# A decoder layer with two mixers: twenty pairs of weight columns formed by seven block products in a stage of their own

## What is computed

```python
h = rms_norm(x, g_norm[l]) * (1.0 + scale) + shift
proj = h @ w_in[l]
xa, va, oa, za, ia, fa, qa, ka, vat, zb, ga, gb = jnp.split(proj, split_at, axis=-1)
xc = silu(causal_depthwise_conv(xa, w_conv[l], b_conv[l]))
q_m, k_m = xc_h @ w_q_mlstm, xc_h @ w_k_mlstm * (MLSTM_HEAD_DIM ** -0.5)
h_m = mlstm_chunkwise(q_m, k_m, v_m, ia + b_igate[l], fa + b_fgate[l])
h_m = rms_norm(sigmoid(oa) * h_m, g_mlstm_head[l]) + skip_mlstm[l] * xc
y_m = (h_m * silu(za)) @ w_out_mlstm[l]
qh, kh = partial_rotary(qa, positions), partial_rotary(ka, positions)
o_g, lse_g = dilated_window_attention(qh, kh, vh, window, dilation)   # 3 groups x 4 heads
o_a = sum over the groups of softmax(lse) * o_g
y_a = (o_a * silu(zb)) @ w_out_attn[l]
merged = sigmoid(ga) * y_m + sigmoid(gb) * y_a
x = rms_norm(x + gate * (merged @ w_out[l]), g_final)
```

## Time and profile before

| | busy in the span of 1565.1 us | share |
|---|---|---|
| TensorE, matmul | 1552.8 us | 99% |
| TensorE, weight load | 1219.1 us | 78% |
| VectorE | 816.0 us | 52% |
| ScalarE | 510.7 us | 33% |
| GpSimd | 368.4 us | 24% |
| DMA | 117.19 MB | 75 GB/s on the mean |

### The profile page before, as it was taken

How to read it: one execution, slowest core, us unless ns; L and a number is a source line. 1 busy time by engine, 2 the same in 40 slices (tenths; PEclk the granted TensorE clock), 3 DMA queues, 4 the chain that set the end, 5 groups by cost and what they waited for, 6 DMA issues and landing times.

```text
span 1565.1 us, 17246 instructions
## 1 busy us (share of the span) xinstructions
PE 1552.8 (99%) x6717; PEld 1219.1 (78%) x6717; DVE 816.0 (52%) x1360; ACT 510.7 (33%) x925; POOL 368.4 (24%) x206
## 2 busy tenths in 40 slices
PE   8999999999999999999999999999999999999998
PEld 7777788877778887777888777788877777777776
DVE  7685446455454645434464543446396415343476
ACT  7644223432322343132235313222542336111122
POOL 0221111122111112211111211111128764221441
PEclk9888888888888888888888888888888888888888
DMA  9211011143111114210001421011041305332432
GB/s 335 93 55 44 27 28 28 35 141 95 61 41 41 41 37 146 67 41 27 28 27 28 136 67 41 27 27 28 28 136 40 121 1 201 100 102 95 158 121 94
DMA packets 51818, 117.19 MB, mean 75 GB/s; under 512 B 20753, under 2 KB 20881, under 8 KB 51734
## 3 DMA queue, kind: packets, MB, share of 16 engines
q1 hardware_dynamic: 47642, 103.23, 20.3%
q10 hardware_dynamic: 2976, 8.80, 1.6%
q0 software_dynamic: 1120, 4.06, 0.9%
HBM read 100.64 MB, written 15.43 MB: 74 GB/s over the span
## 4 chain that ended last, share of the span: by engine, by line
PE 98%; DMA 1%; ACT 1%; SPq 0%; DVE 0%; issue 0%; ACTq 0%; DVEq 0%
PE banks L568 27%; PE banks L567 27%; PE banks L569 27%; PE banks L858 2%; PE banks L868 2%; PE banks L819 2%; PE banks L825 2%; PE banks L877 1%; PE banks L805 1%; PE banks L817 1%; PE banks L558 1%; PE banks L846 1%; PE banks L530 1%; DMA raw_lo<-in_x 1%; PE banks L835 1%; PE banks L807 1%
## 5 line engine op out<-in xcount | busy, mean ns | idle before, releaser
L567 PE MATMUL banks<-h_hi,whi 128*128 128x512 f32 x1000 | 427.8, 428 | 0.4 <-ACT szb L939 0.3
L707 POOL TENSOR_TENSOR wlo<-wraw,whi 128x1024 fp32r<-128x1024 f32 x77 | 194.4, 2524 | 970.8 <-ACT whi L955 952.9
L569 PE MATMUL banks<-h_hi,wlo 128*128 128x512 f32 x1000 | 417.3, 417 | 0.0
L568 PE MATMUL banks<-h_lo,whi 128*128 128x512 f32 x1000 | 417.1, 417 | 0.0
L569 PEld LDWEIGHTS banks<-h_hi,wlo 128*128 128x128 f32 x1000 | 191.9, 192 | 58.6
L567 PEld LDWEIGHTS banks<-h_hi,whi 128*128 128x128 f32 x1000 | 193.0, 193 | 55.2 <-issue 1.2
L568 PEld LDWEIGHTS banks<-h_lo,whi 128*128 128x128 f32 x1000 | 192.8, 193 | 54.1
L955 ACT ACTIVATE whi<-wraw 128x1024 fp32r<-128x1024 f32 x75 | 78.9, 1052 | 97.8 <-PE banks L569 97.8
L568 PE MATMUL banks<-wlo,h_hi 128*128 128x512 f32 x240 | 100.2, 418 | 0.0
L569 PE MATMUL banks<-whi,h_lo 128*128 128x512 f32 x240 | 100.2, 417 | 0.0
L567 PE MATMUL banks<-whi,h_hi 128*128 128x512 f32 x240 | 99.9, 416 | 0.0
(11 more groups left out here) (382 smaller groups left out, 2708.5 us busy)
## 6 DMA issues: line engine op xcount, KB each, us to landing
wraw<-in_w_all SPq DMA_DIRECT2D x92, 512.0 KB, 3.6
s_wada<-in_w_ada_cols SPq DMA_DIRECT2D x16, 512.0 KB, 6.5
raw_lo<-in_x SPq DMA_DIRECT2D x8, 512.0 KB, 9.2
mlstm_branch<-xc SPq DMA_DIRECT2D x8, 512.0 KB, 3.8
qm<-group_weights SPq DMA_DIRECT2D x8, 512.0 KB, 6.2
part<-in_w_ada_gate SPq DMA_DIRECT2D x16, 256.0 KB, 3.4
sig_c<-in_w_all SPq DMA_DIRECT2D x8, 512.0 KB, 4.5
um_lo_raw<-mlstm_branch SPq DMA_DIRECT2D x8, 512.0 KB, 4.9
```

The lines of the kernel that those rows point to most:

```text
L567: t_.matmul(out, w_hi, x_hi, start=first, stop=False)
L568: t_.matmul(out, w_hi, x_lo, start=False, stop=False)
L569: return t_.matmul(out, w_lo, x_hi, start=False, stop=last)
L707: nc.gpsimd.tensor_tensor(wlo[:, hi, :], wraw[:, q % 2, :], whi[:, hi, :].bitcast(F32), ALU.subtract).then_inc(w_split, 1)
```

## The change

A new stage, `blocks`, stands between `setup` and `mix`. In it 20 pairs of weight columns are formed by seven block products each: the 5 gates m = 3 to 7, the 12 pairs of query and key (one for each attention head), and the 3 conv inputs of the heads 1 to 3. The conv input of head 0 and the gate m = 2 are made plainly ahead of them; the gates m = 0 and 1 stay in the merge. TensorE has 7 x 12 = 84 matmuls of 512 columns for it. GpSimd has 4 combinations and 7 splits for a pair, ScalarE 7 roundings, 1 copy and 2 final copies, VectorE 7 additions, and for a query and key pair the rotation of 32 partitions for both at once. A result of 1 MB goes through `fin` to DRAM (`sig_d`, `qk_d`, `xa_d`), and the heads and the merge load it from there.

A head now has 10 chunks (4 of tokens, 3 of values, 2 of ZA, 1 of ZB) and the fold. The small matmuls stand behind each group of 12 matmuls: 24 steps u per head from the first value chunk on, with the mLSTM from u = 3, the attention from u = 5, the normalisation at u = 19 and the turning of the output at u = 21. The `sums` and the rope tables are made in `blocks`, and what the heads use comes later or earlier in the program accordingly.

```diff
-MAIN = 18
...
+VO, VG, ZA, ZB = 0, 4, 7, 9
+MAIN = 10
...
+PRODUCTS = 7
+ORDER = (5, 1, 2, 4, 6, 7, 3)
+PARTS = ("u2", "u4", "c11", "c22", "v", "c21", "c12")
+GATES = KT - PLAIN - 1
+QK0 = GATES
+XA0 = QK0 + HEADS * GROUPS
+PAIRS = XA0 + HEADS - 1
+TOTAL = PRODUCTS * PAIRS
...
+def blocks(nc, a, sem, ps, T):
...
+        def load_pair(r):
+            if r == 0:
+                sp.wait_ge(w_split, 6)
+            elif r >= 2:
+                sp.wait_ge(s_split, PRODUCTS * (r - 1))
+                sp.wait_ge(s_added, 4 * (r - 1))
+            for c in range(2):
+                sp.dma_start(raw[r % 2][:, c, :], a["w_all"][PAIRS0 + 2 * r + c]).then_inc(pair_in[r % 2], 16)
+
+        def store(r):
+            sp.wait_ge(fin_done, 2 * r + 2)
+            sp.dma_start(dest(r), fin[:, r % 2]).then_inc(fin_out[r % 2], 16)
...
+        def combine(j, x, y, op):
+            nc.gpsimd.tensor_tensor(sum_at[j], x, y, op).then_inc(s_added, 1)
+
+        def low(r, j):
+            o = at_product(r, j)
+            pool.wait_ge(s_high, o + 1)
+            nc.gpsimd.tensor_tensor(wlo4[:, o % 4, :], source(r, j), whi4[:, o % 4, :].bitcast(F32), subtract).then_inc(s_split, 1)
...
+        for r in range(PAIRS):
+            pool.wait_ge(pair_in[r % 2], 32 * (r // 2 + 1))
+            if r:
+                pool.wait_ge(s_split, PRODUCTS * r)
+            combine(5, quarter(r, 1, 0), quarter(r, 1, 1), add)
+            pool.wait_ge(s_added, made(r, 5))
+            low(r, 5)
+            combine(6, sum_at[5], quarter(r, 0, 0), subtract)
+            pool.wait_ge(s_added, made(r, 6))
+            combine(3, quarter(r, 0, 1), sum_at[6], subtract)
+            combine(7, quarter(r, 0, 0), quarter(r, 1, 0), subtract)
+            pool.wait_ge(s_added, made(r, 7))
+            for j in ORDER[1:]:
+                low(r, j)
...
+        def product(r, j):
+            o = at_product(r, j)
+            bank_free(o)
+            pe.wait_ge(s_split, o + 1)
+            if r == 0 and j in factor_ready:
+                pe.wait_ge(t_lo_done, factor_ready[j])
+            hi, lo = factors[j]
+            for k in range(KH):
+                cols = slice(k * P, (k + 1) * P)
+                mm = three_pass(t_, bank(r, j), whi4[:, o % 4, cols], wlo4[:, o % 4, cols], hi[:, k, :], lo[:, k, :],
+                                k == 0, k == KH - 1)
+            mm.then_inc(gprod, 1)
...
+        for o in range(TOTAL):
+            r, j = o // PRODUCTS, ORDER[o % PRODUCTS]
+            if j == 1:
+                keep_first(r)
+            if o + 4 < TOTAL:
+                weight_high(o + 4)
+            if r and j == ORDER[4]:
+                finalise(r - 1)
+            if (r, j) == (2, ORDER[0]):
+                rope_tables()
...
+        def join(r):
+
+            c11, c12, c21, c22 = (c_sum[:, r % 2, j, part] for j in range(2) for part in (LEFT, RIGHT))
+            dve.wait_ge(first_kept, r + 1)
+            plus(r, "u2", c21, c11, 6)
+            plus(r, "u4", c12, c21, 5)
+            plus(r, "c11", c11, c11, 2)
+            plus(r, "c22", c22, c12, 7)
+            plus(r, "v", c21, c21, 7)
+            plus(r, "c21", c21, c21, 4)
+            plus(r, "c12", c12, c12, 3)
+
+        def rope(r):
+
+            flat = lambda x: x.rearrange("p j s -> p (j s)")
+            x = c_sum[0:ROPE, r % 2]
+            dve.wait_ge(part_added, PRODUCTS * (r + 1))
+            step(v.stream_shuffle(flat(rot[:]), flat(x), [(m + ROPE // 2) % ROPE for m in range(ROPE)]))
+            step(v.tensor_tensor(rot[:], rot[:], sinT[:].unsqueeze(1).broadcast_to([ROPE, 2, S]), ALU.mult))
+            step(v.tensor_tensor(x, x, cosT[:].unsqueeze(1).broadcast_to([ROPE, 2, S]), ALU.mult))
+            v.tensor_tensor(x, x, rot[:], ALU.add).then_inc(roped, 1)
...
-                if p in (11, 14, 16):
-                    save_stats(i, (11, 14, 16).index(p))
-                if p == 17:
-                    turn_stats(i)
...
-                if n == 1:
-                    next_high(2)
-                    fold_high()
-                    conv_sigmoid(0)
...
-                if n == 14:
-                    rstd()
-                if n >= ZA:
-                    z_sigmoid(n)
...
+    POINTS = 4 * (MAIN - VG)
+    SCORES, ATTEND, NORM, TURN = 3, 5, 19, 21
+
+    def mlstm_step(u):
+
+        return u - SCORES if SCORES <= u < SCORES + 2 * NCH else None
+
+    def attend_step(u):
+        return divmod(u - ATTEND, 6) if ATTEND <= u < ATTEND + 6 * GROUPS else None
...
+                if p == 10:
+                    save_stats(i, 2)
+                    turn_stats(i)
...
+            for n in range(VG, MAIN):
+                for h in range(2):
+                    for half in range(2):
+                        project(n, h, half)
+                        if (n, h, half) == (VG, 0, 1):
+                            head_q()
...
+                        mixing(4 * (n - VG) + 2 * h + half)
...
+            def mixing(u):
+                m, at = mlstm_step(u), attend_step(u)
+                if m is not None and m % 2:
+                    inter((m - 1) // 2)
+                if at:
+                    attend(*at)
+                if m is not None and m % 2:
+                    square((m - 1) // 2)
+                if u == NORM:
+                    rstd()
...
+            conv_sigmoid(0)
+            fold_next()
+            next_high(2)
+            xc_high(0)
+            conv_sigmoid(1)
+            next_high(3)
+            xc_high(1)
+            next_high(4)
+            for j in range(4):
+                keep_tokens(1, j)
+            next_high(5)
+            for j in range(4):
+                keep_tokens(0, j)
+            fold_high()
+            for n in range(VG, MAIN):
+                for h in range(2):
+                    for half in range(2):
+                        if half:
+                            keep(n, h)
+                            if h:
+                                next_high(n + 2)
+                                if n >= ZA:
+                                    z_sigmoid(n)
```

1364 lines of the change are left out of this document (625 added, 739 removed).

## The result

The changed kernel takes 1481.5 us (median of 4 runs, 1478.2 to 1484.0) against 1421.8 before: slower by 4.2%, ratio 1.0419 with a 95% interval of 1.0401 to 1.0436. Forecast was 1447, in a range of 1408 to 1466.

The account below looks back on a forecast made before the run. The prediction took TensorE's issue of products as the bound. For the runs it summed 1422.4 - 38.2 (products) + 24.0 (A) + 3.9 (B) + 22.8 (C) + 4 (D) + 5 (E) + 3 (F) = 1446.9 us, range 1408 to 1466.

Parts of the forecast that it names:

- The products removed: 14 more pairs by blocks, 168 products fewer on TensorE: 38.2 us less in the runs, 1384.2 us without new waits.
- A: Start of heads 1 to 3: TensorE waits for the third token chunk's split, 8.0 us each, 24.0 in the runs.
- F: The rest: head query waiting for the fold, and less cover for splits at the merge: 3 us in the runs (0 to 9).
- B: First head, from the last block product through store, load, convolution and split: wait of 3.9 us in the runs (0 to 8).
- C: Normalisation in four heads: exponentials and normalised output late behind ScalarE's row of work, 22.8 us in the runs (20 to 28).
- D: Block stage: VectorE's rope and GpSimd block each other in 12 pairs, mostly hidden: 4 us in the runs (0 to 29).
- The rule of the Trainium skill: VectorE instructions with two SBUF inputs contend with GpSimd's SBUF reads, the blocked one waiting throughout; 29 us for D.
- E: Start of the block stage: the third product's rounding stands behind three gate functions, 5 us in the runs (0 to 8).
- The port bounds: Rival, 8 in 100: block-stage VectorE and GpSimd never overlap, D at its upper bound of 29 us, 1472 us.
- its condition: The port rival decides when both engines' 21.5 us per pair exceeds its 84 products and nothing is left to shift.
- what was to show it: Sign of the port rival: TensorE waits on GpSimd in every pair of the block stage.

Follow-up runs that it names:

- number 12: norm_split_22 with za's second sigmoid on ScalarE behind step u = 21 instead of u = 19: 1413.5 us, ratio 0.9940 to the kernel before.
- Number 3: Changed kernel with only za's two sigmoids on ScalarE moved behind the step of mixing instead of ahead of it: 1466.2 us, ratio 1.0316.
- experiment 6: Changed kernel without the rotation of query and key in the block stage: 1460.9 us, ratio 1.0270.
- 5: Changed kernel with the block stage's start reordered, one more rounding ahead of the gates' logarithms, rotation angles one pair later: 1477.6 us.
- the first two kernels of 10: Changed kernel with head starts reordered on ScalarE and VectorE, za's sigmoids later, turning at u = 22: 1442.1 us; with the block stage's start reordered too: 1435.2 us.
- number 1: Changed kernel with only ScalarE's order at a head's start changed, roundings ahead of the conv sigmoids: 1491.5 us, ratio 1.0493.
- norm_split_22: Changed kernel with heads, block-stage start and pairs reordered, VectorE's normalisation cut in two, output turned at u = 22: 1426.4 us, ratio 1.003.

## Why the prediction was wrong

The way was right, slower, and the size too small: 59.7 us slower instead of 24.5. By its own steps:

*The products removed* (38.2 us, and 1384.2 us with no new wait) were right to about 5 us. The list of waits of number 12's kernel adds up to 29.2 us, that of the kernel before to 5.7, nearly all in the setup. Without the 23.5 us more its profiled execution (1411.3) would have taken 1388 and its median 1390.

*A, the start of heads 1 to 3*: 8.0 us each in the runs. Measured 8.3, 6.8 and 7.4, plus 5.4 us at half clock, which no term had. The chain was right to the step. What I did not see is that a second one, through VectorE and the load of ew, was as late: F had 3 us for it and the merge together (9 at most), and when the first wait was taken away it was 10.7 to 10.9 us a head. Without both the heads are 32 us faster.

*B*: 3.9 forecast (its pieces add up to 25.4 and not 25.7, so 3.6), 3.1 measured. *C*: 22.8 forecast. The waits are 16.5 us (the output 8.0, exponentials 6.0, ew 2.5). Exponentials and ew together are the 2.1 us a head of the sum; the output has 1.4 us in three heads and 3.0 in one where the sum had 3.1 in each. In three heads a stretch at half clock stands among them (833 to 845: clock 0.86 on the mean, 1.6 us lost). That makes 21. That the size is right is luck: the clock, which no term had, took what I overrated in the waits. Number 3 gave 15.3 of it back, and the kernel of number 12 has 0.3 us of these waits left.

*D* is the step that failed: "Most of it disappears: 4 us in the runs (0 to 29)". It cost 20.6 us by experiment 6. The bound had been worked out well (21.5 us a pair by turns, 21.2 measured), and the reason for not taking it was wrong: being ahead by four products helps once, not in twelve pairs in a row that each need 2 us more than TensorE. The trace shows it: nothing is waited for at the first rotation (213), 0.7 us at the second (232.07), 1.7 us at the third (253.30), and from then on the same pattern repeats. An estimate from the prediction's own numbers: 29 us less a lead of at most four products, 4 x 2.73 = 10.9, is 18 to 29 in the sum and 1461 to 1472 in the forecast. The rule of the Trainium skill that the prediction weighed ("SBUF — State Buffer", Who interferes with whom) gave the right bound and the right mechanism (rounds of 3.3 us, above), and the trace of before had one row for it, which I took for an exception.

*E*: 5 forecast. The wait is 11.2 us and at half clock follow 9 products from 97.43 to 101.41, 4.0 us instead of 2.0. My chain had the three gate functions on ScalarE but took VectorE's sums ahead of them as done. They end at 84.6, and ScalarE begins the gate functions at 86.8 and the rounding at 94.4, when TensorE has stood since 86. Of the last six sums the four beside GpSimd's operations took 2.31 us each, the two after them 1.21. So a part of this wait, 4.4 us of VectorE's time, has the same cause as D; that the rest follows from it is not shown. Of E 4 to 7 us come back by order (5, and the step between the first two kernels of 10).

*F*: 1.6 us measured in the list, at the merge, 3 forecast.

*The clock* is the second step that failed: the sum has no term for it. Every wait was priced by its length alone, and 12 us were lost at 1.2 GHz behind the waits of the profiled execution (A 5.4, C 4.8, E 2). D alone does not explain the miss: with 20.6 in place of 4 the forecast would have been 1463.5, inside its range. The missing clock and E's 11.2 in place of 5 take it out.

Together 28 + 3 + 21 + 21 + 13 + 2 = 88 on top of 1384 give 1472; the profiled execution took 1478, the median 1481.5. Of the 3 us between the last two the listed clocks (0.985 and 0.979) point at more time at 1.2 GHz. The other 6 are not assigned.

Of the rivals the mechanism of "The port bounds" (8 in 100) came true; its condition was the one that decides, and what was to show it was right too: waits for GpSimd in every pair from the third on. Its number, 1472, was not met: D cost 20.6 us and not 29, and the 9.5 us up to 1481.5 lie in other terms.

## What to carry to other kernels

Work that is moved into one long run of equal items must be judged by the mean of each engine over such an item; where rows show that VectorE's and GpSimd's work takes turns, as here, the two are added up, not laid side by side, and a few slots of lead only delay the bill. A wait on an engine that is otherwise full also costs the products at the lower clock behind it, here 1.6 to 2.1 us. A wait that is found says nothing of the chains behind it: before an order is changed for one engine, work out when the next consumer's other inputs are ready, or the fix can cost more than it gives (number 1, +10 us; with VectorE's order as well, -32). The same holds for a wait that is moved (norm_split_22, +4.8). And a mixed order is only as good as its last item.

## What the hardware showed

TensorE's clock fell to its lower level (1.2 GHz; a product of 512 columns then took 0.43 us, not 0.23) during or behind waits of 6.8 to 11.2 us, and also in three of four heads behind waits of 0.6 and 1.4 us close together; in the changed kernel 1.6 to 2.1 us were lost each time. It did not fall every time: in the last head, with waits of 0.6, 1.4 and 3.0 us, it stayed up, and behind the first head's wait of 3.1 us it stayed up in the changed kernel and fell in number 3. With the waits gone the mean granted clock rose from 0.985 to 0.996. One execution of the kernel before ran at 0.851 from 15 us to its end, with no wait but one of 0.3 us, while its timed runs had 0.997 to 1.000: nothing here shows why. A shuffle of 32 x 2048 elements (2.56 us) left GpSimd alone (its operations of 128 x 512 elements stayed at 1.29 us). Two-operand work on the same elements did not (3.33 us for GpSimd's, 3.3 for VectorE's), nor did a tensor_scalar (2.3 and 2.2 us).
